# The gather by place in rounded products, with the splits and five remainders on GpSimd

## The reference

```python
def hier_moe(h, w_rg, b_rg, w_re, b_re, w_gate, w_up, w_down):
    g_logits = (xf @ w_rg + b_rg)            # 4 groups, one is taken
    g_sel = jnp.argmax(g_logits, axis=-1)
    ...
    top_v, top_i = lax.top_k(e_in_group, 2)  # 2 of its 8 experts
    ...
    for e in range(32):
        hid = jax.nn.silu(xf @ w_gate[e]) * (xf @ w_up[e])
        y = y + combine[:, e:e + 1] * (hid @ w_down[e])
```

## Time and profile before

| | |
|---|---|
| median of 3 runs | 1446.83 us |
| profiled execution | 1447.46 us |
| its span | 1445.7 us |
| PE busy | 1421.4 us (98%) |
| DVE busy | 1152.6 us (80%) |
| ACT busy | 836.2 us (58%) |
| POOL busy | 41.4 us (3%) |
| granted PE clock, mean | 0.998 |

### The profile page before, as it was taken

How to read it: one execution, slowest core, us unless ns; L and a number is a source line. 1 busy time by engine, 2 the same in 40 slices (tenths; PEclk the granted TensorE clock), 3 DMA queues, 4 the chain that set the end, 5 groups by cost and what they waited for, 6 DMA issues and landing times.

```text
span 1445.7 us, 23081 instructions
## 1 busy us (share of the span) xinstructions
PE 1421.4 (98%) x8086; PEld 1231.3 (85%) x8086; DVE 1152.6 (80%) x2046; ACT 836.2 (58%) x1312; POOL 41.4 (3%) x64
## 2 busy tenths in 40 slices
PE   8999999999999999999999999999999999999998
PEld 6777888999988888878788888898888898888886
DVE  5985579898989888796889788769888785698786
ACT  6566656888775444467874444546444386654343
POOL 5100000000011000000000000000000000000000
PEclk9999999999999999999999999999999999999999
DMA  9745344999978666562447666457666652476661
GB/s 271 211 138 189 126 131 141 344 344 338 341 256 229 198 194 188 175 195 61 132 140 224 180 198 190 146 160 213 181 194 194 181 158 75 123 228 188 190 192 54
DMA packets 262571, 275.00 MB, mean 190 GB/s; under 512 B 10832, under 2 KB 212864, under 8 KB 262496
## 3 DMA queue, kind: packets, MB, share of 16 engines
q1 hardware_dynamic: 259520, 268.45, 60.6%
q0 software_dynamic: 2976, 5.58, 1.6%
HBM read 272.86 MB, written 1.06 MB: 189 GB/s over the span
## 4 chain that ended last, share of the span: by engine, by line
PE 91%; DVE 4%; ACT 3%; issue 1%; DMA 0%; SPq 0%; DVEq 0%; ACTq 0%
PE ps L810 18%; PE ps L727 16%; PE ps L729 16%; PE ps L728 16%; PE ps L814 11%; PE ps L815 3%; PE ps L1503 1%; DVE w_lo L2412 1%; PE ps L844 1%; ACT w_hi L1800 1%; PE ps L1689 1%; PE ps L1412 1%; PE ps L856 1%; ACT xT_both L1809 1%; PE ps L757 1%
## 5 line engine op out<-in xcount | busy, mean ns | idle before, releaser
L2412 DVE TENSOR_TENSOR w_lo<-raw,w_hi 128x1024 fp32r<-128x1024 f32 (+3 forms) x311 | 369.2, 1215 | 43.8 <-ACT w_hi L1800 41.9
L1800 ACT ACTIVATE w_hi<-raw 128x1024 fp32r<-128x1024 f32 (+3 forms) x311 | 315.2, 1049 | 25.5 <-PE ps L729 20.1
L810 PE MATMUL ps<-xT_both,w_hi 128*128 128x512 f32 x1120 | 281.8, 391 | 0.0
L1873 ACT ACTIVATE w_hi<-raw 128x1024 fp32r<-128x1024 f32 x198 | 208.6, 1058 | 115.0 <-PE ps L729 102.8
L810 PEld LDWEIGHTS ps<-xT_both,w_hi 128*128 128x128 f32 x1120 | 210.5, 188 | 42.1
L2417 DVE TENSOR_TENSOR w_lo<-raw,w_hi 128x1024 fp32r<-128x1024 f32 x198 | 236.0, 1220 | 0.8
L1868 ACT ACTIVATE hid_sil<-hid_sil 128x256 f32<-128x256 f32 x90 | 37.6, 419 | 264.7 <-DVE hid_sil L2481 236.6
L814 PEld LDWEIGHTS ps<-xT_both,w_lo 128*128 128x128 f32 x1280 | 174.4, 190 | 12.2
L814 PE MATMUL ps<-xT_both,w_lo 128*128 128x256 f32 x1280 | 178.8, 283 | 0.0
L727 PE MATMUL ps<-w_hi,hid_hi 128*128 128x512 f32 x432 | 170.7, 395 | 1.2 <-DVE hid_lo L3035 0.7
L729 PE MATMUL ps<-w_hi,hid_lo 128*128 128x512 f32 x432 | 169.1, 391 | 0.0
(11 more groups left out here) (490 smaller groups left out, 2408.2 us busy)
## 6 DMA issues: line engine op xcount, KB each, us to landing
raw<-in_ffn_w_gate_dram SPq DMA_DIRECT2D x88, 512.0 KB, 4.2
raw<-in_ffn_w_up_dram SPq DMA_DIRECT2D x88, 512.0 KB, 5.3
raw<-in_ffn_w_down_dram SPq DMA_DIRECT2D x88, 512.0 KB, 4.3
raw<-in_w_in_dram SPq DMA_DIRECT2D x40, 512.0 KB, 4.7
raw<-in_w_gate_dram SPq DMA_DIRECT2D x40, 512.0 KB, 5.0
raw<-in_w_up_dram SPq DMA_DIRECT2D x40, 512.0 KB, 5.4
raw<-in_w_down_dram SPq DMA_DIRECT2D x40, 512.0 KB, 5.2
raw<-in_rg_w_in_dram SPq DMA_DIRECT2D x16, 512.0 KB, 4.5
```

Of the source, the lines that this page charges most:

```text
L810: pe.matmul(o, hi[:, k, :], both[:, :, k, :], start=k == 0, stop=False)
L1800: act.activation(w_hi[0:parts, i % RING, 0:cols], raw[0:parts, i % RING, 0:cols], ACT.Copy)\
L1873: act.activation(w_hi[:, s, :], raw[:, s, :], ACT.Copy).then_inc(hi_done, 1)
L2412: dve.tensor_tensor(w_lo[0:parts, s, 0:cols], raw[0:parts, s, 0:cols], w_hi[0:parts, s, 0:cols].bitcast(F32), ALU.subtract).then_inc(lo_do ...
```

## The change

The residual is split as the weights are: POOL copies `x_res` into the rounded `xr_hi` (laid over `xn`) and subtracts to get `xr_lo` (over `sq`). `place` becomes a rounded tile; its ones and zeros are exact. The gather multiplies `xr_hi` and `xr_lo` by `place`, in rounded form, two products for one of before. PE waits for `xr_ok` ahead of it. POOL also makes the remainders of five pieces, b+5, V, V+1, V+3 and V+4 (`POOL_LO`), which DVE made. DVE waits for each (`pool_lo`) and counts `lo_done` itself, so that the counter keeps its order; V+1's wait now stands behind `xs_remainder(0)`. The new counters share semaphores of earlier stages (`AGAIN`).

```diff
-        place = ar(7680, NT * T).rearrange("p (t c) -> p t c", t=NT)
+        place = over("place", [NT, T], F32R, "arena", 7680)
+
+        xr_hi = over("xr_hi", [NT, D], F32R, "xn", 0)
+        xr_lo = over("xr_lo", [NT, D], F32R, "sq", 0)
...
+        POOL_LO = [PLAN.start["moe"] + 5] + [PLAN.start["visit"] + q for q in (0, 1, 3, 4)]
...
+            for t in range(NT):
+                pool.wait_ge(x_part, X_PART[1] + t)
+                pool.wait_ge(x_ready, X_AT[1] - 1 + t)
+                pool.tensor_copy(xr_hi[:, t, :], x_res[:, t, :]).then_inc(sig("xr_hi_ok"), 1)
+            for t in range(NT):
+                pool.wait_ge(norm_ssq, R_AT[1])
+                pool.wait_ge(*nth("xr_hi_ok", t + 1))
+                pool.tensor_tensor(xr_lo[:, t, :], x_res[:, t, :], xr_hi[:, t, :].bitcast(F32), ALU.subtract)\
+                    .then_inc(sig("xr_ok"), 1)
+
+            for i in POOL_LO:
+                pool.wait_ge(hi_done, i + 1)
+                q = i % RING
+                pool.tensor_tensor(w_lo[:, q, :], raw[:, q, :], w_hi[:, q, :].bitcast(F32), ALU.subtract)\
+                    .then_inc(sig("pool_lo"), 1)
...
                 pe.wait_ge(*nth("place_ok", 1))
+                pe.wait_ge(*nth("xr_ok", 2))
                 sorted_x(0, 4)
...
-                        v = x_res[:, t, :].rearrange("p (c k) -> p k c", k=KT)
-                        m = pe.matmul(ps[:, bank, (k % 2) * T:(k % 2 + 1) * T], v[:, k, :], place[:, t, :],
-                                      start=t == 0, stop=t == 1)
+                        for x in (xr_hi, xr_lo):
+                            v = x[:, t, :].rearrange("p (c k) -> p k c", k=KT)
+                            m = pe.matmul(ps[:, bank, (k % 2) * T:(k % 2 + 1) * T], v[:, k, :], place[:, t, :],
+                                          start=t == 0 and x is xr_hi, stop=t == 1 and x is xr_lo)
...
+            def pool_lo(i):
+
+
+                dve.wait_ge(*nth("pool_lo", POOL_LO.index(i) + 1))
+                dve.sem_inc(lo_done, PLAN.step(i))
...
-            lo(b + 5)
+            pool_lo(b + 5)
             unweighted(0, b + 3, 1)
             unweighted(1, b + 5, 7)
-            lo(V)
+            pool_lo(V)
...
-            lo(V + 1)
             xs_remainder(0)
-            lo(V + 3)
+            pool_lo(V + 1)
+            pool_lo(V + 3)
             dve.wait_ge(sig("comb01_ok"), 1)
             weighted(0)
...
             weighted(1)
-            lo(V + 4)
+            pool_lo(V + 4)
```

More of the change, by code:

```diff
@@ L258, in two_blocks @@
                  "rank_diag": "kdec_ok", "place_ok": "state_ok", "route_ok": "og_ok", "table_ok": "qkn_ok",
-                 "cw_ok": "qaT_ok", "ctl_ok": "ki4_ok", "rank_row_ok": "alT_ok", "xs_hi_ok": "l_ok"}
+                 "cw_ok": "qaT_ok", "ctl_ok": "ki4_ok", "rank_row_ok": "alT_ok", "xs_hi_ok": "l_ok",
+                 "xr_hi_ok": "silr_ok", "xr_ok": "gla_sq", "pool_lo": "lam_abs"}
         def sig(name):
@@ L1330, in table_products @@
                     for t in range(NT):
-                        m = pe.matmul(ps[:, 3, 160 + 13 * tile:173 + 13 * tile], place[:, t, tile * P:(tile + 1) * P],
+                        m = pe.matmul(ps[:, 3, 160 + 13 * tile:173 + 13 * tile], place[:, t, tile * P:(tile + 1) * P].bitcast(F32),
                                       route[:, t, 0:13], start=t == 0, stop=t == 1)
```

## The result

The changed kernel takes 1459.88 us, the median of four runs (1458.78 to 1461.08), against 1446.87 us for the kernel before beside it: a ratio of 1.009, 95% interval 1.0078 to 1.0102. The forecast was 1445.6 us with a range up to 1452.4, so the time lies outside it, on the slow side. The profiled execution took 1459.53 us with a span of 1457.7, 12.0 above that of before.

The account below looks back on a forecast made before the run. PE, busy 98%, was taken as the bound, with DVE close behind: dense down 1.87 us early less 0.70 for V+4 gives 1.17, so 1447.46 - 1.2 = 1446.26, against the median 1445.6 us; 8-in-10 range 1443.6 to 1452.4.

Parts of the forecast that it names:

- cost nothing while that cover lasts: POOL's subtractions for xr_lo, b+5 and V, from about 215.7 us, end before PE or DVE needs them: no cost.
- without holding DVE: Main forecast's condition: POOL subtractions of 1.2 to 2.6 us leave DVE's instructions unhindered; chance 0.50, 1445.6 us.
- 7.6 us of slack: Spare time of POOL's four early subtractions, from 215.7 us until DVE wants V's remainder at about 232.1.
- rival 1: POOL subtractions hold DVE's two-SBUF-operand instructions in the chain ending in place, five holds of 1.8 us: 1453.1; chance 0.27.
- lead of 1.2: Net gain of 1.17 us at PE's gap at 250.97: 1.87 early at dense down less 0.70 late from V+4.
- the landmark: PE's last gap of note, at 250.97 us before the change, waiting for DVE's hid_lo; forecast near 249.8.
- the forecast lead: First dense down product on PE starts at 238.87 instead of 240.74 us, 1.87 early.
- Rival 3: On PE, the strided load sets the gather's pace, 32 loads at 0.246 us, no quicker: +0.7, 1447.5 us; chance 0.07.
- the free end: Strided gather load on PE costs nothing extra: 0.12 us a rounded product, in a range of 0.12 to 0.246.
- V+3's remainder: POOL ends it at 236.83 us; DVE waits for it before weighted(0), setting the dense down start at 238.87.
- V+4's wait: DVE waits about 1 to 2.5 us for POOL ahead of pass 0's product, making hid_lo 0.70 us late.
- Rival 4: An extra POOL instruction ahead of its first subtraction delays it; 15 us would give +2.3, 1449.1 us; chance 0.06.

Follow-up runs that it names:

- a_splits_only: Changed kernel with the five remainders back on DVE, POOL keeping only the residual's split; 1452.5 us, ratio 1.0035.
- e_early_splits: Remainders on DVE, each POOL split subtraction directly behind its cast, xr_lo in its own buffer, against the changed kernel; 1449.03 us, ratio 1.0013.
- d_memsets: Changed kernel with each of POOL's seven subtractions replaced by a zero fill of the same tile, for timing only; 1449.14 us, ratio 1.0011.
- b_remainders_only: Changed kernel without the split, gather in plain float32 as before, POOL making the five remainders; 1451.87 us, ratio 1.003.
- c_contiguous_view: Changed kernel with the gather's fixed operand read without a stride (other channels), for timing only; 1459.01 us, ratio 1.0075.
- h_memsets_contiguous: Changed kernel with zero fills for POOL's seven subtractions and the gather's operand read without a stride; 1446.31 us, ratio 0.999.
- k_warm_alone: `f_early_contiguous` plus five plain filler products on PE behind the table products; 1446.46 us, ratio 0.9998.
- f_early_contiguous: `e_early_splits` with POOL writing the split tiles so that the gather's fixed operand is contiguous; 1448.28 us, ratio 1.0005.
- j_later_and_warm: `i_later_remainder` plus three plain filler products on PE behind the table products; 1445.9 us, ratio 0.9993.
- i_later_remainder: `f_early_contiguous` with DVE's remainder of V+3 moved from ahead of weighted(0) to behind weighted(1); 1446.73 us, ratio 0.9997.

## Why the prediction was wrong

**The step that failed.** It is the sentence on the early subtractions, "cost nothing while that cover lasts", and the forecast's condition, POOL "without holding DVE". The 7.6 us of slack were counted in time between POOL's end and the first reader of its result; the price was paid in DVE's small instructions beside it. That is rival 1, to which I gave 0.27. Its mechanism is shown by `a_splits_only` (two subtractions, two holds), `e_early_splits` (the same two over other work, none) and `d_memsets`. The rival's condition, two operands in SBUF, was too narrow: L2994 in the changed kernel and L2903 in `b_remainders_only` have one tensor operand and are held as well. The Trainium skill's page SBUF — State Buffer, section Who interferes with whom, states it so: whoever has the shared ports keeps them for a whole instruction. The trace agrees, 2.10 to 2.32 us for an instruction of 0.16.

**Rival 1's size.** It gave 1453.1, and the kernel takes 1459.88. In its sum, held time was 5 x 1.8 = 9.0 less 1.5 of slack. Measured, it is those five subtractions that hold, for 10.06 us in all, so h was 2.0. What the sum missed lies behind the gather's start: it left the lead of 1.2 in, as if the gather were quicker.

- From the gather's start to the dense down products the forecast had 238.87 - 229.50 = 9.37 us. Before it was 11.24, after it is 14.49. That is 5.12 us over the forecast.
- From there to the landmark: 10.23 before, 10.93 by the forecast (0.70 later), 12.81 after, 1.88 over.

The two make 7.0; the gather's start is 6.39 late, where the rival had 9.0 - 1.5 = 7.5 for all five holds, the fifth of which lies behind that start. So -1.2 + 7.0 + 6.4 = 12.2, the landmark's lateness. 0.60 of the 6.39 is no part of the change: it is there at the residual's sum.

PE's timelines show where the 7.0 lie. Up to the dense down products, 1.87 is the forecast lead itself, which a gather as slow as before can't give. Of the 3.25 over before, 0.37 lie in the first half; 1.10 between it and the next quarter (240.19 to 241.95, against 233.43 to 234.09), where PE is idle for 0.18 and 0.94 us for DVE, late by the fifth hold; 0.95 and 0.76 in the small products behind the two quarters (244.18 to 246.18 against 236.21 to 237.26, and 248.26 to 250.38 against 239.38 to 240.74), where the clock is at its lower level. Behind that start, the dense down products take 1.26 longer at the lower clock (4.34 against 3.08), and the 1.32 up to the landmark hold two waits of PE for DVE, 0.86 and 0.79, behind DVE's wait for V+4, for which the forecast had 0.70 in all. This is read from the trace; no single experiment divides it, since the causes cover each other.

**The gather.** Rival 3 was true as well, at 0.07: 0.24 us a product, not 0.12. I had chosen the free end by the transposes of the earlier trace rows, 0.14 a record; the row of the very loads in question, stood for the other end. With the contiguous view the term is right at 0.12 (`c_contiguous_view`).

**POOL's rate.** 2.35 to 2.39 us a subtraction where I took 2.2, and a range of 0.87 to 2.62. The estimate from the Trainium skill's page GPSIMD Engine Reference, section Elementwise side-by-side, was 2.25, which is nearer. By this the start of the dense down products would be 0.2 later; it didn't matter.

**V+3 and V+4.** V+3's remainder was not the path that the forecast made of it. POOL ends it at 246.63, but `weighted(0)` starts at 246.92, released by ACT's copy of the combining weights, which had waited for PE's late small products and ends at 246.29 + 0.60 = 246.89:

```profile
246.29 0.60 ACT L2184 ACTIVATE arena<-ps 128x512 f32<-128x512 f32 x1 [2.08 <-PE ps L1479]
```

The table's copy then waits for PE (1.43 us in its row at 250.09), and so it is PE's own late work that sets the start of the dense down products. Only in `b_remainders_only` does `weighted(0)` wait for V+3's remainder, 2.40 us. V+4's wait is where it was expected and longer: POOL ends it at 258.50 and DVE goes on at 258.64, after 4.11 us of waiting, where I had named 1 to 2.5.

**Rival 4.** POOL's own instruction ahead of its first subtraction shows no cost. The subtraction starts at 216.37, 0.09 behind the second square's last row on ACT (216.03 + 0.25). The Trainium skill's page GPSIMD Engine Reference, section Instruction dispatch, gives about 6 us for the first call of a freshly loaded library. Between POOL's last cast and this subtraction lie 3.00 us of idle time, which could have held them only in part, so no row here shows them.

**The clock.** No term of the sum had it. It was 1.00 everywhere before, and I took the 0.12 of a quicker PE for granted without asking what a PE that then waits is granted. In `h_memsets_contiguous` 2.4 us of lead are gone within the stretch whose clock is at the lower level. Where filler products alone kept it at 1.00, that gave back 1.12 us (`k_warm_alone` against `f_early_contiguous`) and 0.58 (`j_later_and_warm` against `i_later_remainder`).

## What to carry to other kernels

Ask of work given to GpSimd not only when its result is needed, but what VectorE runs beside it. Long two-operand work on GpSimd belongs beside VectorE's PSUM reads (here 207 to 215 us), not beside a chain of 0.16 us instructions in SBUF, each of which can cost a whole GpSimd instruction. A product that is made cheaper pays only if its load is cheaper too and PE is not left waiting at the end of it. And before two traces are compared, count both from a row ahead of the change: 1.01 us of difference upstream hid the 1.14 us that `i_later_remainder` gained.

## What was not expected of the hardware

- A fill by GpSimd, which reads nothing, held VectorE's one-operand TENSOR_SCALAR and COPY from SBUF to SBUF (0.99 instead of 0.29 us, 0.68 instead of 0.16), and no two-operand instruction. A subtraction held both kinds (2.55 us for a pair of TENSOR_SCALAR that took 0.36 before).
- Where VectorE's own two-operand work had begun first, GpSimd was held (3.10 instead of 2.37 us, `b_remainders_only`).
- A rounded 128x128 load with a stride of eight elements sets a pace of 0.24 us a product, a contiguous one 0.12; the plain 32-bit gather had the first of the two already.
- The granted clock fell to 0.50 with PE busy 4.00 of 4.00 us in the window before (`e_early_splits`); only rounded products at 0.24 us each, with strided loads, stood ahead of it. Plain products at the same pace kept it at 1.00 (`b_remainders_only`, and before). That such products are the cause is argued, not shown.
- POOL's cast of 128x1024 took 1.04 us, and 2.05 to 2.09 with both sides strided; its subtraction 2.40 and 2.92 to 2.99.
